# Weight blocks of 512 KB instead of 1 MB, and ten instead of eight row buffers for the gathered expert rows

## What is computed

```python
def peer_ffn(x, w_query, sub_keys, expert_down, expert_up):
    ...
        top_s, sel = lax.top_k(cand, PEER_TOPK)
        eidx = jnp.take_along_axis(cidx, sel, axis=-1)
        g = jax.nn.softmax(top_s, axis=-1)
        u = expert_down[eidx]
        vv = expert_up[eidx]
        act = jax.nn.gelu(jnp.einsum('td,thkd->thk', xc, u).astype(jnp.float32), approximate=False)
        return jnp.einsum('thk,thkd->td', (g * act).astype(x.dtype), vv)
```

## Time and profile before

| | |
|---|---|
| median of 3 runs | 3145.93 us (3140.52 to 3148.44) |
| the profiled execution | 3139.5 us, its span 3137.6 us |
| busy of the span | PE 2681.7 us (85%), DVE 1604.0 (51%), POOL 999.6 (32%), ACT 602.4 (19%) |
| moved by DMA | 817 MB, 549 of them by POOL's queue (the gathers), 266 by SP's (the stream) |
| stages | first block, layer 0: dense to 335 us, PEER to 1125; layer 1: dense to 1450, PEER to 2290; second block to the end |

### The profile page before, as it was taken

How to read it: one execution, slowest core, us unless ns; L and a number is a source line. 1 busy time by engine, 2 the same in 40 slices (tenths; PEclk the granted TensorE clock), 3 DMA queues, 4 the chain that set the end, 5 groups by cost and what they waited for, 6 DMA issues and landing times.

```text
span 3137.6 us, 28943 instructions
## 1 busy us (share of the span) xinstructions
PE 2681.7 (85%) x9764; PEld 1788.0 (57%) x9764; DVE 1604.0 (51%) x3671; ACT 602.4 (19%) x1272; POOL 999.6 (32%) x1040
## 2 busy tenths in 40 slices
PE   7898977987879788998779998967676899977999
PEld 6466733533435355677336665733254788845888
DVE  1531467988877525314788777678626100044100
ACT  2241112322120012411123331021022200122100
POOL 0000366665666610002566664566700000000000
PEclk9899999999989998999889999988886899967999
DMA  6445699998999954456899999999920344411344
GB/s 249 148 161 215 251 376 367 409 383 328 373 363 404 410 215 147 152 194 265 320 361 411 412 411 364 379 383 364 396 81 14 107 149 159 147 41 67 134 157 152
DMA packets 187291, 817.45 MB, mean 261 GB/s; under 512 B 20592, under 2 KB 22656, under 8 KB 154128
## 3 DMA queue, kind: packets, MB, share of 16 engines
q0 software_dynamic: 148784, 549.31, 45.4%
q1 hardware_dynamic: 38368, 266.35, 23.2%
HBM read 814.54 MB, written 1.05 MB: 260 GB/s over the span
## 4 chain that ended last, share of the span: by engine, by line
PE 53%; DVE 17%; POOL 10%; issue 9%; DMA 5%; another core or an unknown queue 4%; ACT 1%; DVEq 0%; ACTq 0%; SPq 0%; POOLq 0%
PE work L589 45%; PE acc L589 7%; DVE arena L1615 6%; POOL arena L547 5%; POOL arena L572 5%; DMA arena<-experts_down,arena 3%; DVE arena L1464 2%; DMA ring<-stream 1%; DVE arena L1644 1%; PE work L663 1%; DVE arena L1568 1%; DVE arena L1569 0%; DVE arena L1571 0%; DVE arena L1570 0%
## 5 line engine op out<-in xcount | busy, mean ns | idle before, releaser
L589 PE MATMUL acc<-arena 128*128 128x512 f32 x1824 | 914.5, 650 | 269.6 <-issue 155.3
L589 PE MATMUL work<-arena,ring 128*128 128x256 f32 x3460 | 767.9, 384 | 32.2 <-ACT arena L1395 14.5
L589 PEld LDWEIGHTS acc<-arena 128*128 128x128 f32 x1824 | 365.6, 207 | 747.5 <-issue 588.5
L572 POOL DMA_INDIRECT arena<-experts_down,arena x512 | 495.5, 968 | 851.3 <-DVE arena L1599 662.3
L589 PEld LDWEIGHTS work<-arena,ring 128*128 128x128 f32 x3460 | 666.5, 193 | 138.2 <-issue 26.3
L1615 DVE SCALAR_TENSOR_TENSOR arena<-arena,acc 128x1024 f32<-128x1024 f32 x512 | 610.2, 1217 | 161.5 <-DMA arena<-experts_down,arena 85.5
L547 POOL DMA_INDIRECT arena<-experts_up,arena x512 | 496.9, 971 | 400.3 <-PE acc L589 148.9
L589 PE MATMUL work<-h,ring 128*128 128x256 f32 x1440 | 338.0, 394 | 11.1 <-issue 9.8
L589 PEld LDWEIGHTS work<-h,ring 128*128 128x128 f32 x1440 | 281.2, 198 | 66.5 <-issue 27.3
L589 PE MATMUL work<-lent,ring 128*128 128x256 f32 x992 | 224.3, 379 | 0.0
L589 PEld LDWEIGHTS work<-lent,ring 128*128 128x128 f32 x992 | 188.5, 190 | 52.5 <-issue 30.1
(11 more groups left out here) (230 smaller groups left out, 1651.0 us busy)
## 6 DMA issues: line engine op xcount, KB each, us to landing
ring<-stream SPq DMA_DIRECT2D x252, 1024.0 KB
arena<-experts_down,arena POOLq DMA_INDIRECT x512
arena<-experts_up,arena POOLq DMA_INDIRECT x512
arena<-na_bias POOLq DMA_DIRECT2D x2, 2048.0 KB, 15.0
arena<-consts POOLq DMA_DIRECT2D x1, 2392.0 KB
lent<-consts POOLq DMA_DIRECT2D x2, 1024.0 KB
arena<-consts POOLq DMA_DIRECT2D x1, 1816.0 KB
x<-x_in SPq DMA_DIRECT2D x1, 1024.0 KB, 5.7
```

What stands on the lines that cost most here:

```text
L572: pool.indirect_dma_start(down[:, (l * PICKS + n) % ROWS, :], None, experts[2 * l], bass.IndirectOffsetOnAxis(ap=expert[:, n:n + 1], axis=0))\
L589: ins = nc.tensor.matmul(o, w, r, start=start, stop=stop, **kw)
```

## The change

`BT` goes from 16 to 8, so that a block is 512 KB and the ring of four holds 2 MB. The 16 KB per partition that this frees go to the arena (`ARENA`), where `ROWS` rises from 8 to 10 for down and up. So that the 32 tiles of `ws` can be waited for block by block, they are collected in the loop of the first token tile. The rows add six semaphores, and six others are merged into two names (`zeroed`, `c2_loaded`) with the same order of events.

```diff
-BT = 16
+BT = 8
 RING = 4
...
-ROWS = 8
+ROWS = 10
...
-ARENA = 30432
+ARENA = 34528
...
-            pool.memset(sc_t[:, :, :], 0.0).then_inc(sem("sc_zero"), 1)
+            pool.memset(sc_t[:, :, :], 0.0).then_inc(sem("zeroed"), 1)
...
-                            pool.dma_start(c2_c, consts2[:, 0:C2_CONTEXT]).then_inc(sem("c2_c_loaded"), 16)
+                            pool.dma_start(c2_c, consts2[:, 0:C2_CONTEXT]).then_inc(sem("c2_loaded"), 16)
...
-            pe.wait_ge(sem("c2_loaded"), 16)
+            pe.wait_ge(sem("c2_loaded"), 48)
...
-                ws = [tiles(TM_WIDE) for _ in range(KD)]
+                ws = []
                 for t in range(TT):
                     n = N_TM2 * P
                     b = bank(f"tm{l}", t)
                     for k in range(KD):
+                        if t == 0:
+                            ws.append(tiles(TM_WIDE))
                         mm(b[:, 0:n], h2[:, k, t * P:(t + 1) * P], ws[k][:, 0:n], k == 0, k == KD - 1,
                            inc=bank_full if k == KD - 1 else None)
                 read(KD * TM_WIDE)
```

More of the change, by code:

```diff
@@ L533, in _ @@
         def _(pool):
-            pool.memset(sc_t[:, :, :], 0.0).then_inc(sem("sc_zero"), 1)
+            pool.memset(sc_t[:, :, :], 0.0).then_inc(sem("zeroed"), 1)
             pool.dma_start(c1[:, :], consts1[:, 0:C1_FIXED]).then_inc(sem("c1_loaded"), 16)
             pool.dma_start(lent[:, :], consts1[:, C1_FIXED:C1_N]).then_inc(sem("lent_loaded"), 16)
-            pool.memset(glu_c[:, :, :], 0.0).then_inc(sem("glu_c_zero"), 1)
+            pool.memset(glu_c[:, :, :], 0.0).then_inc(sem("zeroed"), 1)
             for l in range(DEPTH):
@@ L579, in _ @@
             copied(pool, f"ytr{DEPTH - 1}", 2 * TT - 1)
-            pool.memset(glu[:, :, :], 0.0).then_inc(sem("glu_zero"), 1)
+            pool.memset(glu[:, :, :], 0.0).then_inc(sem("zeroed"), 1)
         @block.tensor
@@ L906, in context_mixers @@
                             copied(pe, "cfm", N_FM2 - 1)
-                            pe.wait_ge(sem("c2_c_loaded"), 16)
+                            pe.wait_ge(sem("c2_loaded"), 16)
                             for a in range(2):
@@ L1139, in _ @@
             A.need("c1_loaded", 16)
-            A.need("sc_zero", 1)
+            A.need("zeroed", 1)
             A.step(f(sc_t[:, :, 0:2], k1("cond").rearrange("p (k s) -> p k s", s=2), ACT.Silu), "cond_silu")
@@ L1372, in _ @@
                             A.step(f(y_row[:, o], y_acc[:, o], ACT.Copy), f"y_row{l}")
-            A.need("c2_loaded", 16)
+            A.need("c2_loaded", 48)
             for l in range(DEPTH):
@@ L1689, in context_mixers @@
                         if beat == 2:
-                            V.need("c2_c_loaded", 16)
+                            V.need("c2_loaded", 16)
                             scales_c(gs1_c, "g1", 0, 1, c2_c)
@@ L1698, in context_mixers @@
                             n = (beat - 17) // 2
-                            V.need("glu_c_zero", 1)
+                            V.need("zeroed", 2)
                             copied(dve, "cfm", 2 + n)
@@ L1752, in context_rest @@
                         elif beat == 79:
-                            V.need("c2_v_loaded", 16)
+                            V.need("c2_loaded", 32)
                             scales_c(gs1_c, "g1", 1, 1, c2_v)
@@ L1785, in _ @@
                 add_up(TT - 1)
-            V.need("c2_loaded", 16)
+            V.need("c2_loaded", 48)
             for l in range(DEPTH):
@@ L1800, in _ @@
                 normalise_tokens(f"norm2_{l}", gs1, f"hs2_{l}")
-                V.need("glu_zero", 1)
+                V.need("zeroed", 3)
                 for n in range(2):
```

2 lines of the change are left out of this document (1 added, 1 removed).

## The result

| same chip, interleaved | before | after |
|---|---|---|
| median of 4 runs, us | 3147.18 (3140.52 to 3151.69) | 3194.02 (3190.62 to 3195.47) |
| ratio | 1 | 1.0152 (95%: 1.0133 to 1.0170) |
| span of the profiled execution, us | 3137.6 | 3192.2 |
| first to last gather, layer 0 / layer 1 | 769.1 / 820.9 | 779.4 / 821.0 |
| first gather of layer 0; last of layer 0 to first of layer 1; last gather to the end | 339.3; 343.4; 864.9 | 358.3; 364.0; 869.5 |

The forecast was 3148 us, within 3121 and 3174. The dense stages of the first block (ahead of the first gather, and between the last gather of layer 0 and the first of layer 1) took 19.0 + 20.6 us more, where the forecast had some 22, and PEER got 10 us longer instead of 22 shorter. These 10 us must be read with care: the profiled execution of before (3139.5 us) lies 7.7 us under its median, that of after (3194.14) at its median.

A forecast was written before the change was run, and what follows sets the result against it. PE was taken to bound the dense stages; PEER's bound changed between bandwidth, PE, DVE and POOL's gather chain. Stream +24 less rows 22 gave +2 us on 3139.5, or 3148 us against the median 3145.93, range 3121 to 3174.

The forecast's parts named there:

- +3.4 us a burst: Modulation bursts HEADS, MERGE, FFN in both layers: the halved ring lengthens each by 3.4 us, six by 20.4.
- the other four at the rate of the wires: In a burst: after the first missing block at 4.80 us, four more land 1.28 us apart, the last at 9.92.
- The bound of 6.1: Upper bound of a burst's cost in us, if a 512 KB block took 4.84 us and the last waited for its slot.
- `NORM` of layer 1: +2, from 0 to 3.4: Modulation burst already waiting 5.14 us beside the 2 MB of na_bias: 2 us longer with the halved ring.
- Sum of the stream: Whole cost of the halved ring, bursts 20.4, NORM 2 and 0, tm 1.8: +24 us, from 17 to 44.
- The rows: 22 us, bounds 0 and 55: PEER's gather stages: ten buffers instead of eight save 22 us, about two thirds of a counted 35.
- two picks more in flight let POOL run on: POOL's gathers in PEER: POOL runs 2 x 2.48 = 4.97 us past the point where it stands today.
- The bandwidth bound of 55 us: PEER stages below 411 GB/s and full of neither DVE nor PE: reaching that rate saves at most 55 us together.
- A loss I exclude: PEER and query stage: earlier gathers competing with the stream cost nothing, as three blocks ahead cover 15 and 10.3 us.
- The rival of 3167 us: DVE's ranking and PE bound most of layer 0: rows give 5 us, bursts cost 26, +21; chance 0.27.
- The rival of 3193: 512 KB stream blocks come one at a time, 0.15 us more for each of some 300 dense blocks, 45 us; chance 0.03.
- `tm`: Product of 32 tiles, which fill the new ring: its fourth block comes 0.9 us late, twice, 1.8 us, from 0 to 3.6.

The follow-up runs named there:

- e3: after, but each modulation block is freed by its own last matmul, not by the next block's first matmul: 3080.9 us, 1.0042 of before.
- e1: after with eight row buffers instead of ten, so the stream's half of the change alone: 3107.5 us, 1.0128 of before.
- the late gate: POOL's wait for the last ranking score at pick 22 instead of 16: after with it 1.0042 of before, the same with eight rows 1.0113.
- e12: before with gathers of half the bytes, except the first eight picks of a layer: 3125.84 us against 3151.14, 0.9922.
- b_before: before unchanged, profiled once more on the second, faster chip: 3068.6 to 3069.4 us there.
- b_after: after unchanged, on the second, faster chip: 3103.5 us, 1.0112 of before.
- e2: before with 512 KB blocks, eight of them (4 MB ring as before), and eight rows: 3046.8 us, 0.9925 of before.
- e6: before with six row buffers of each kind in use instead of eight, on the first chip: 3153.1 us, 1.0000 of before.
- e8: 512 KB blocks, eight of them, eight rows, each modulation block freed by its own last matmul: 3046.6 us, 0.9927 of before.

## Why the prediction was wrong, point by point

Two terms failed, both to the slow side: the stream's bursts, `NORM` among them, cost twice what was forecast, and the rows gave 4 us of 22.

- **"+3.4 us a burst": mis-sized, 6.3 to 6.6.** The six bursts took 38.6 us more, where the forecast had 20.4. The size of the first landing was right (4.76 and 4.83 us into the burst, for 4.80). The failed step is "the other four at the rate of the wires": it took for granted that all four slots are in flight. The late release leaves three, and `e3` shows it. But it gives back 1.9 us of a burst, not the whole gap of about 3. With its own release a burst still costs 4.3: the last block comes 10.3 us into it in the burst shown and 11.4 in `MOD_FFN` of layer 0, for 9.92, and why these landings are slower than the wires is open. The bound of 6.1 had been worked out for a block of 4.84 us that waits for its slot, the right mechanism under the wrong condition.
- **"`NORM` of layer 1: +2, from 0 to 3.4": mis-sized, 6.0.** It lasts 16.51 us instead of 10.50. `NORM` of layer 0 took 1.7 more, for 0. These two are the rest of the 47.2 us: the single steps last 1.00 us at most, in before and in after, so "nothing" was right for them.
- **Sum of the stream: +24 forecast, +38.9 measured (`e1`)**, inside the 17 to 44 that the prediction gave for it (its own upper bounds, 36.6 + 3.4 + 2 + 3.6, add up to 45.6).
- **The rows: 22 us, bounds 0 and 55.** The size fits another kernel: 26.0 us with the late gate (22 to 26 by how it is read), 4.0 with the early one. On the first chip the rows were not run by themselves. There the whole change cost 46.8 us, on the second 34.4; PEER makes the difference (+10 against -13.4 us), and why is open. The failed step is "two picks more in flight let POOL run on". The 4.97 us are there once the gate is late (5.0 at pick 24 of each layer); with the early gate they are lost at pick 16. The step was applied to every stall in the earlier trace rows and to the entry of layer 1, but the gate was not among the waits that were read, though the wait of pick 16 (3.56 us, up to 406.90) stood just ahead of the window that begins at 411. With two more picks in flight, POOL meets it 11 us earlier.
- **The range.** Its upper end, 3174, took a cost of 33 and a gain of 5, though the prediction's own bounds were 44 and 0. With a cost of 38.9 and a gain of 4, both inside the bounds, the same sum gives 3181; the first chip measured 3194. That both terms could fail to the same side was not in the range.
- **The bandwidth bound of 55 us** was refuted (`e12`): it assumed that a stage at 411 GB/s has nothing behind it. The stage has PE 4% behind.
- **"A loss I exclude" (the query stage).** On the first chip PE's waits without a named releaser, from the first gather to the end of that stage, went from 4.1 to 8.0 us. On the second chip there are none, with the full ring (`b_before`) or with the short one (`e1`, `b_after`). So the exclusion holds there, and what made the 4 us on the first chip is open.
- **The rival of 3167 us** ("the bursts remain, the stalls too") named the right side, but not the reason: its rows gave little because DVE and PE would be the bound. What took more than half of their gain was the gate. The rival of 3193 gave the number that was measured, by a mechanism that is not there: the SwiGLU shows no wait and `e2` none of the loss. That it fits is luck, and a right number is no evidence for its story.
- **Right:** landing waits of the dots under 10 us (9.8), the SwiGLU unchanged, the wait of a burst split over several records, the dense stages of the first block as the place of the loss, and `tm`. Its fourth block is missing after 12 of 32 records, and the two `tm` take 11.26 and 11.38 us instead of 10.48, +1.7 for a forecast of 1.8. The first of them, in after:

```profile
2380.61 4.03 PE L589 MATMUL work<-ring,arena 128*128 128x384 f32 x12
2385.15 6.72 PE L589 MATMUL work<-ring,arena 128*128 128x384 f32 x20 [0.51 <-DMA ring<-stream]
```

## What to carry to other kernels

Give a slot back with its own last reader, not with the next instruction: that one may wait for the slot's successor, and the ring is one shorter exactly when it runs dry. In a ring of bytes, smaller blocks at equal bytes are cheap to try (-22 us here); fewer bytes are not. Before paying for deeper buffers, list every wait on the producer's queue, also those that cost little today: a gate that costs 3.6 us because the producer is late anyway took 15.8 when it was early, and kept back more than half of what the buffers give (13 of 24 us in the gather spans). The experiment that took buffers away (`e6`) could not show it: with six rows POOL has no wait at the gate at all.

## What was not expected of the hardware

From SyncE's issue to the first matmul that uses it a block of 512 KB took 3.61 us in after and 3.74 in `e8`, one of 1 MB 4.84 in before: half the bytes save a quarter. (The median landing of all 504 blocks of `e2` is 3.7 us.) The Trainium skill's page "DMA: Bandwidth & Descriptors", section "Anatomy of one DMA", would give 3.2 us for the small one (an estimate from the page). But the section's formula is for DMAs that GpSimd issues, and SyncE issues the stream, so these figures don't test it. The prediction set it beside the stream too; nothing in its sum rests on it.

Behind a burst PE runs for a while at a lower granted clock. Windows behind the burst `HEADS` in after and, below, in before, both on the first chip (columns as above; 1.00 is 2.4 GHz, and 0.5 would be 1.2 throughout):

```profile
111.00:123.00 12.00, 5.58 (x16) 2.77 (x14) 7.20 (x13) 0.78 (x2) 0.00 (x0) 0.64 0.26 90
123.00:137.00 14.00, 10.18 (x35) 6.83 (x36) 4.42 (x12) 4.48 (x11) 0.00 (x0) 0.62 0.02 10
```

```profile
106.00:118.00 12.00, 4.32 (x14) 1.89 (x13) 8.31 (x14) 1.78 (x3) 0.00 (x0) 0.78 0.64 236
118.00:134.00 16.00, 13.33 (x50) 8.95 (x51) 4.39 (x13) 5.52 (x16) 0.00 (x0) 0.71 0.18 58
```

In after 26 us at a mean of 0.63, in before 28 us at 0.74. But PE also stands idle for half of the first window or more in each of these kernels, and on the second chip the same stretch has 0.64 in `b_before`, 0.71 in `e2` and 0.76 in `e8`. So before has the low clock too, and that the longer burst of after deepens it is not shown. Over the whole execution the difference is small (mean granted clock 0.914 against 0.920 before, on the first chip), and the matmuls of the steps have a median of 617 ns where before has 592 (in both the slowest is 1062). What it costs by itself was not separated.

The two kinds of chip differ by 2.5% for the same kernel. In the traces of before the gather spans are 83 us longer on the slower one and everything else together 13.5 us shorter. The gain of the late gate in after is smaller on the slower one (0.5% against 0.7%), a difference within the spread of the runs.
